# Idle products first, TensorE's and VectorE's early work in another order, and one weight split on GpSimd: a transformer stack on one core

## The reference

```python
z = (xn @ w_in).astype(jnp.float32)          # xn: x after rms_norm
q = z[..., :512]; k = z[..., 512:1024]; v = z[..., 1024:1536]   # per head of 64
u = z[..., 1536:]
q = partial_rope(q, positions) * (HEAD_DIM ** -0.5)
k = partial_rope(k, positions)
att = dilated_attention(q, k, v)
ssm = s5_mixer(u, a_re, a_im, log_dt, b_re, b_im, c_re, c_im, d_skip, w_glu)
y = jnp.concatenate([att, ssm], axis=-1)
return y @ w_out

# in s5_mixer, for 32 groups of 16 inputs and 64 complex states:
a_bar = jnp.exp(A * dt)
b_bar = ((a_bar - 1.0) / A)[..., None] * lax.complex(b_re, b_im)
bu = jnp.einsum('gpc,bsgc->bsgp', b_bar, u)
h = associative_scan over s of  h = a_bar * h + bu
y = jnp.einsum('gcp,bsgp->bsgc', c_mat, h).real + d_skip * u
y = gelu(y);  return y * sigmoid(y @ w_glu)
```

## Time and profile before

| what | value |
|---|---|
| median of 3 runs | 1249.65 us (1249.41 to 1251.18) |
| span of the profiled execution | 1248.4 us, first to last instruction |
| TensorE (PE) busy | 1236.7 us, 99% |
| VectorE (DVE) busy | 811.4 us, 65% |
| ScalarE (ACT) busy | 668.3 us, 54% |
| GpSimd (POOL) busy | 89.2 us, 7% |

### The profile page before, as it was taken

How to read it: one execution, slowest core, us unless ns; L and a number is a source line. 1 busy time by engine, 2 the same in 40 slices (tenths; PEclk the granted TensorE clock), 3 DMA queues, 4 the chain that set the end, 5 groups by cost and what they waited for, 6 DMA issues and landing times.

```text
span 1248.4 us, 15780 instructions
## 1 busy us (share of the span) xinstructions
PE 1236.7 (99%) x6366; PEld 1031.4 (83%) x6366; DVE 811.4 (65%) x1037; ACT 668.3 (54%) x965; POOL 89.2 (7%) x121
## 2 busy tenths in 40 slices
PE   7999999999999999999999999999999999999998
PEld 6778888888888888888888888888888888888887
DVE  7995756654788766554687746656547785655553
ACT  7865653433898654443687535444436644544431
POOL 2410000000100100000232000000001300000000
PEclk9999999999999999999999999999999999999999
DMA  7344555555554565555554235555555315555551
GB/s 306 105 140 144 190 198 172 199 173 199 189 200 163 192 222 183 192 179 200 181 199 169 68 102 169 202 192 179 184 192 181 131 39 202 199 186 185 183 188 67
DMA packets 32536, 216.60 MB, mean 173 GB/s; under 512 B 3904, under 2 KB 4544, under 8 KB 7376
## 3 DMA queue, kind: packets, MB, share of 16 engines
q1 hardware_dynamic: 30384, 210.32, 48.8%
q0 software_dynamic: 1360, 4.78, 1.2%
q10 hardware_dynamic: 720, 0.50, 0.1%
HBM read 214.54 MB, written 1.05 MB: 173 GB/s over the span
## 4 chain that ended last, share of the span: by engine, by line
PE 93%; DVE 4%; issue 1%; DMA 1%; ACT 0%; SPq 0%; DVEq 0%; ACTq 0%
PE PS L461 26%; PE PS L463 26%; PE PS L462 26%; PE PS L467 6%; PE PS L791 2%; PE PS L815 1%; PE PS L496 1%; PE PS L498 1%; PE PS L495 1%; PE PS L544 1%; PE PS L538 1%; PE PS L539 1%; DVE WL L1748 1%; DMA X<-in_x 1%; DVE YG L2037 1%
## 5 line engine op out<-in xcount | busy, mean ns | idle before, releaser
L1748 DVE TENSOR_TENSOR WL<-RAW,WH 128x2048 fp32r<-128x2048 f32 (+2 forms) x200 | 442.9, 2218 | 310.6 <-ACT WH L1130 310.6
L1130 ACT ACTIVATE WH<-RAW 128x2048 fp32r<-128x2048 f32 (+2 forms) x200 | 371.2, 1858 | 366.4 <-PE PS L463 366.1
L461 PE MATMUL PS<-WH,HTh 128*128 128x512 f32 (+1 forms) x848 | 334.6, 395 | 0.2
L463 PE MATMUL PS<-WH,HTl 128*128 128x512 f32 (+1 forms) x848 | 329.0, 388 | 0.0
L462 PE MATMUL PS<-WL,HTh 128*128 128x512 f32 (+1 forms) x848 | 328.3, 387 | 0.0
L463 PEld LDWEIGHTS PS<-WH,HTl 128*128 128x128 f32 x848 | 159.2, 188 | 33.2
L461 PEld LDWEIGHTS PS<-WH,HTh 128*128 128x128 f32 x848 | 159.4, 188 | 32.0 <-DVE WL L1748 0.8
L462 PEld LDWEIGHTS PS<-WL,HTh 128*128 128x128 f32 x848 | 159.5, 188 | 30.6
L461 PE MATMUL PS<-WH,YAh 128*128 128x512 f32 x402 | 158.6, 394 | 0.1
L463 PE MATMUL PS<-WH,YAl 128*128 128x512 f32 x402 | 156.7, 390 | 0.0
L462 PE MATMUL PS<-WL,YAh 128*128 128x512 f32 x402 | 156.5, 389 | 0.0
(11 more groups left out here) (354 smaller groups left out, 1442.9 us busy)
## 6 DMA issues: line engine op xcount, KB each, us to landing
RAW<-in_w SPq DMA_DIRECT2D x196, 1024.0 KB, 4.9
BC<-in_rows POOLq DMA_DIRECT2D x4, 512.0 KB, 4.0
YG<-in_mem POOLq DMA_DIRECT2D x4, 512.0 KB, 4.7
X<-in_x SPq DMA_DIRECT2D x2, 512.0 KB, 5.4
RAW<-in_w SPq DMA_DIRECT2D x4, 256.0 KB, 6.0
BC<-in_s SPq DMA_DIRECT2D x1, 512.0 KB, 11.6
YG<-in_s SPq DMA_DIRECT2D x1, 512.0 KB, 11.9
BB<-in_s SPq DMA_DIRECT2D x1, 512.0 KB, 12.5
```

Of the source, the lines that this page charges most:

```text
L461: e.matmul(out, ah, bh, start=start, stop=False)
L463: return e.matmul(out, al, bh, start=False, stop=stop)
L1130: e.activation(WH[:, c % NW, w], RAW[:, c % NR, w], ACT.Copy).then_inc(S.hi, 1)
L1748: e.tensor_tensor(WL[:, c % NW, w], RAW[:, c % NR, w], WH[:, c % NW, w].bitcast(f32), SUB).then_inc(S.lo, 1)
```

## The change

- **Idle products.** VectorE first sets 128x512 of YBh to 1.0 (S.warm). TensorE multiplies it into bank 7 nine times before the first turn and five times behind it; nothing reads the result.
- **first_edge in another order.** For chunk 0: the products upper by upper and lower by upper of the first row tile, then both halves of x's second turn, then what needs the weights' lower part, then the second row tile, with lower by upper last; the same for chunk 1.
- **ev_q.** u_turn stands behind k = 3 (it stood behind k = 2), b_turn behind k = 4 (k = 2), b_u(0) behind k = 6 (k = 3).
- **Chunk 3** is issued by SP ahead of YG and BB, copied by ScalarE ahead of the evacuation of u, and split by VectorE ahead of table(0) and late_c. Chunk 4 is issued ahead of cbias.
- **Chunk 4** (POOLED) is split by GpSimd, between row_rsqrt(0) and the CFe operations, signalled by S.plo; VectorE leaves it out, and `wait_lo` takes the place of the waits for S.lo.

The diff, cut to its core:

```diff
+        POOLED = (PLAN["ev_k"][0],)
+        def lo_n(c):
+            return c + 4 - sum(1 for p in POOLED if p <= c)
+        def wait_lo(e, c):
+            if c in POOLED:
+                e.wait_ge(S.plo, POOLED.index(c) + 1)
+            else:
+                e.wait_ge(S.lo, lo_n(c))
...
+            def idle_products(n):
+                for _ in range(n):
+                    e.matmul(PS[:, 7, :], YBh[:, 0, 0:128], YBh[:, 0:2, :].rearrange("p a b -> p (a b)"), start=True, stop=True)
...
             def first_edge():
...
+                def hi(t, k):
+                    ts, w = slice(128 * t, 128 * t + 128), slice(512 * (k % 4), 512 * (k % 4) + 512)
+                    e.wait_ge(S.hthi, htlo_n(0, t, k))
+                    e.matmul(PS[:, t, :], HTh[:, k, ts], WH[:, k // 4, w], start=k == 0, stop=False)
+                def lo(t, k):
+                    ts, w = slice(128 * t, 128 * t + 128), slice(512 * (k % 4), 512 * (k % 4) + 512)
+                    return e.matmul(PS[:, t, :], HTh[:, k, ts], WL[:, k // 4, w], start=False, stop=t == 0 and k == 7)
+                def rest(t, k):
+                    ts, w = slice(128 * t, 128 * t + 128), slice(512 * (k % 4), 512 * (k % 4) + 512)
+                    e.wait_ge(S.htlo, htlo_n(0, t, k))
+                    return e.matmul(PS[:, t, :], HTl[:, k, ts], WH[:, k // 4, w], start=False, stop=t == 1 and k == 7)
                 for k in range(4):
+                    e.wait_ge(S.hi, k + 1)
+                    hi(0, k)
+                    rest(0, k)
+                e.wait_ge(S.c_x1, 16)
+                turn(0, 1)
+                for k in range(4):
+                    e.wait_ge(S.lo, k + 1)
+                    lo(0, k)
+                for k in range(4):
+                    hi(1, k)
+                    lo(1, k)
+                for k in range(4):
+                    tk = rest(1, k)
                 tk.then_inc(S.used, 1)
+                e.wait_ge(S.hi1, 1)
+                for k in range(4, 8):
+                    if k == 6:
+                        e.wait_ge(S.hi, 5)
+                    hi(0, k)
+                    rest(0, k)
+                for k in range(4, 8):
+                    if k == 4:
+                        e.wait_ge(S.lo1, 1)
+                    elif k == 6:
+                        e.wait_ge(S.lo, 5)
+                    lo(0, k)
+                for k in range(4, 8):
+                    hi(1, k)
+                    lo(1, k)
+                for k in range(4, 8):
+                    tk = rest(1, k)
                 tk.then_inc(S.used, 1)
...
+            e.wait_ge(S.warm, 1)
+            idle_products(9)
             e.wait_ge(S.c_id, 16)
             e.wait_ge(S.c_x0, 16)
             turn(0, 0)
+            idle_products(5)
             first_edge()
...
-            rows_mm(PLAN["ev_q"], 4, 8, 512, HT, (2, 3), at={2: [u_turn, b_turn], 3: [b_first]})
+            rows_mm(PLAN["ev_q"], 4, 8, 512, HT, (2, 3), at={3: [u_turn], 4: [b_turn], 6: [b_first]})
...
             angles(0)
+            feed(PLAN["ev_u"][0])
             e.wait_ge(S.rs, RSTD["row0"])
             evac_in("ev_u", (0, 1), Qn)
-            feed(PLAN["ev_u"][0])
             pairs(0, uT, (4, 5))
...
+                    if n in POOLED:
+                        continue
...
+            e.memset(YBh[:, 0:2, :].bitcast(f32), 1.0).then_inc(S.warm, 1)
...
             late_b()
+            feed(PLAN["ev_u"][0])
             table(0)
-            late_c(lambda: feed(PLAN["ev_u"][0]))
-            rotate(0, lambda: feed(PLAN["ev_u"][1]))
+            late_c()
+            rotate(0)
+            feed(PLAN["ev_u"][1])
             table(1)
...
             row_rsqrt(0)
+            c = POOLED[0]
+            e.wait_ge(S.hi, c + 4)
+            e.tensor_tensor(WL[:, c % NW, :], RAW[:, c % NR, :], WH[:, c % NW, :].bitcast(f32), SUB).then_inc(S.plo, 1)
             e.wait_ge(S.pd, PD["CF"])
...
                 if c >= NR:
-                    e.wait_ge(S.lo, c + 1)
+                    wait_lo(e, c - NR)
...
             e.dma_start(tt[:, :], A["tab"][:, 640:896]).then_inc(S.c_t, 16)
+            weights(3)
             e.dma_start(YG[:, 0, :], A["s5"][:, 2048:3072]).then_inc(S.c_C, 16)
             e.dma_start(BB[:, :, :, :], A["s5"][:, 0:1024].rearrange("p (r q s) -> p r q s", r=2, q=4)).then_inc(S.c_B, 16)
+            weights(4)
             e.dma_start(cbias[:, :, :], A["tab"][:, 128:640].rearrange("p (t k) -> p t k", t=2)).then_inc(S.c_m, 16)
-            for c in range(NR, NCH):
+            for c in range(5, NCH):
                 weights(c)
```

More of the change, by code:

```diff
@@ L225 @@
     c_c c_id c_x0 c_x1 c_p c_i c_t c_B c_C c_m c_S c_bc c_tb c_gr c_mem c_o0 c_o1
-    fills half fin turn hthi htlo x yg sq var rs hi2 rowsq hsq
+    warm plo fills half fin turn hthi htlo x yg sq var rs hi2 rowsq hsq
     rsx th sg an fold yhi ylo
@@ L514, in first_edge @@
-                for i in range(4):
-                    e.wait_ge(S.lo, i + 1)
-                    e.matmul(PS[:, 0, :], HTh[:, i, 0:128], WL[:, 0, 512 * i:512 * i + 512], start=False, stop=False)
-                for k in range(4):
-                    tk = edge_product(0, 0, PS[:, 1, :], 1, k, slice(512 * k, 512 * k + 512))
-                tk.then_inc(S.used, 1)
[L520 to L526, removed]
+                def hi(t, k):
+                    ts, w = slice(128 * t, 128 * t + 128), slice(512 * (k % 4), 512 * (k % 4) + 512)
+                    e.wait_ge(S.hthi, htlo_n(0, t, k))
+                    e.matmul(PS[:, t, :], HTh[:, k, ts], WH[:, k // 4, w], start=k == 0, stop=False)
@@ L535, in rounded @@
                     if k % per == 0:
-                        e.wait_ge(S.lo, c + 4)
+                        wait_lo(e, c)
                     e.wait_ge(S.hthi, htlo_n(ed, 0, k))
@@ L1753, in feed @@
                     n = n_split[0]
+                    n_split[0] = n + 1
+                    if n in POOLED:
+                        continue
                     if ed:
@@ L1758, in feed @@
                     split_lo(n, slice(1024, CH) if ed else slice(0, CH))
-                    n_split[0] = n + 1
             def rest(out, src, hi, gain=None):
@@ L1979, in late_b, with late_c @@
                 e.tensor_tensor(AB[:, 1, :, :], AB[:, 1, :, :], CT_[:, 0, :, :], ADD).then_inc(S.pd, pd.up())
-            def late_c(then):
+            def late_c():
                 e.wait_ge(S.c_C, 16)
@@ L1987, in late_c @@
                 e.tensor_tensor(CT_, CC[:, :, :, :], fi, MUL).then_inc(S.pd, pd.up())
-                then()
                 e.wait_ge(S.pd, PD["f2"])
```

## The result

The change is slower: the median is **1255.12 us** (1254.97 to 1256.61, 5 runs) against 1249.65 us (1249.20 to 1251.18, 5 runs), a ratio of 1.0042 (95% interval 1.0029 to 1.0054), so 5.5 us more. 1254.0 us had been predicted. The profiled spans are 1253.2 and 1248.4 us, 4.8 us apart. On record a time stands 1.75 to 1.95 us above the span of the same execution, so the profiled execution before took some 1250.2 us, half a us more than the median: the medians are further apart than the spans. The ratios leave out three slow executions of over 1370 us, one of the kernel with small CFe operations and two of the kernel before.

A forecast was written before the change was run, and what follows sets the result against it. The prediction took VectorE's chain without slack, then TensorE, to bound the kernel. Terms +0.9, -2.6, -1.1, +1.1 and +6.1 gave +4.4 us, added to the 1249.65 median: 1254.0 us, range 1248.4 to 1257.0.

The forecast's parts named there:

- Start and ev_q: TensorE's start: idle products raise its clock sooner, ev_q begins at 21.3 instead of 24.34, but b_u(0) ends 0.9 us later.
- The rival without an earlier clock: At the start: idle products don't raise the clock sooner, ev_q stays at 24.3; +7.4 us, 1257.0; chance 0.06.
- The split on GpSimd: Chunk 4's split on GpSimd starts at about 35.0 and takes 3.4 us, so chunk 4 is ready at 38.4.
- my bound of 4.2: Chunk 4's split on GpSimd: four operations of 1.05 us would be 4.2 us, the upper split time in the range.
- TensorE's lead: At ev_k: of the 3.0 us TensorE gains by ev_q, some 1.1 are left after waiting for chunk 4.
- the hold of L2071: VectorE's operation ready at 37.3 (L2027 before) waits until GpSimd finishes chunk 4 at 38.4: +1.1 us.
- The CFe operations: Six GpSimd operations behind chunk 4's split, each between two of VectorE's next, hold up VectorE's chain: +6.1 us.
- The sum: VectorE's chain, L2020 to L2042: b_u(0) +0.9, split gone -2.6, L2522 no longer ahead -1.1, L2027 +1.1, CFe +6.1; together +4.4.
- The wait ahead of c_h(0): c_h(0) needs CFe and W, so TensorE waits some 3 to 4 us ahead of it.
- The rival with free scans: VectorE's scans are not held up, only four CFe operations cost: 2.0 us less, +2.4, 1252.0; chance 0.12.
- The rival without hold-up: GpSimd's operations cost VectorE nothing, TensorE sets the pace: 1248.5, or 1247 with a split of 2.3 us; chance 0.25.
- the relay: VectorE's chain from L2020 (34.12) to the split at 71.03 has no slack, then TensorE takes over; any delay delays the end.

The follow-up runs named there:

- the kernel with small CFe operations: The change with each of the six CFe operations cut to 128x64, the rest of CFe set to zero at the start: 1254.28 us, ratio 1.0035.
- the version above: The change without GpSimd's split, old places in ev_q, GpSimd's CFe and rope work put where VectorE reads PSUM: 1247.40 us, ratio 0.9979.
- the pair with whole and small operations: The change with u_turn, b_turn, b_u(0) at their old places: whole CFe operations 1253.66 us, ratio 1.0030; cut to 128x64 1248.03 us, ratio 0.9984.
- VectorE's split with old and with new places: The change with VectorE splitting chunk 4: u_turn, b_turn, b_u(0) at old places 1249.92 us, ratio 0.9999; at new places 1251.81 us, ratio 1.0022.
- keeping TensorE busy: The change with VectorE splitting chunk 4 and 12 more idle products ahead of ev_k: 1250.63 us, ratio 1.0007.

## Why the prediction was right, step by step

- **Start and ev_q.** ev_q at 21.01 (21.3 predicted), L2064 at 34.97 and GpSimd's start at 34.99 (34.9 to 35.0 and 35.0): right. The clock came up sooner than I took it. The rival without an earlier clock is refuted: it had ev_q at 24.3, and even without idle products it began at 22.59.
- **The split on GpSimd: mis-sized.** I took 3.4 us from the line through two smaller operations, and it took 4.56 (4.56 to 4.63 in the six runs that have it ahead of whole or small CFe operations): twice VectorE's 2.29, above my bound of 4.2 too. The Trainium skill ("GPSIMD Engine Reference", 4.1 Engine selection) states about twice VectorE's time for two inputs; these runs agree with it, and the estimate of 4.6 us that I worked out from it and did not use was right. The line through two small operations did not hold for one four times as large. So nothing of TensorE's lead was left at ev_k, where I had kept 1.1 us, and the hold of L2071 was 2.1 us (37.43 to 39.55, the split's end) instead of 1.1.
- **The CFe operations.** VectorE's own pace from L2071 to W is 8.7 us (the version above), and it took 14.2: held up by 5.5 us, where I had 6.1.
- **The sum** then is 0.9 - 2.6 - 1.1 + 2.1 + 5.5 = +4.8 us; W was 4.7 us late, and so was the split at the end of the chain. The +4.4 came out near it because two errors of 1.0 and 0.6 us had opposite signs: that is luck, though the terms and their order were right. The median moved by 5.5 us. The 0.7 us between that and the spans' 4.8 are not in the sum: I added to the median what I had read from an execution half a us longer than it.
- **The wait ahead of c_h(0)** came, but was 2.2 us in two parts (1.97 for L2085, 0.22 for L2086) and not 3 to 4: TensorE had come to ev_k 1.1 us later than I had it.
- **The rival with free scans** is refuted: two scans took 3.99 us beside CFe, and 2.33 without it, before and in the version above. The rule of the Trainium skill ("SBUF — State Buffer", Who interferes with whom) that two SBUF inputs decide holds for scans too in this trace.
- **The rival without hold-up** is refuted by the pair with whole and small operations, 5.6 us apart in time, and by VectorE's rows beside CFe.
- **Missing in the prediction** was the second path, through direct_terms and ScalarE. In the change it is hidden: direct_terms stood at 45.12, and VectorE's second TN had no idle time before it. It decides once the first path is shortened: of the 1.9 us between VectorE's split with old and with new places (1249.9, 1251.8) keeping TensorE busy brought back 1.2. The prediction had looked at what TensorE's wait costs, not at what its clock does after it.

## What to carry to other kernels

Count work that you give to GpSimd against VectorE's rows too: in these runs an operation with two SBUF inputs on GpSimd cost VectorE nothing while VectorE read PSUM or waited, and held it up where VectorE had two SBUF inputs itself. Look at what is queued behind a moved operation, since here it was the six operations behind the split, not the split, that cost most. And a lead that one engine wins is worth what the next engine in the relay can take over: the new start brings TensorE to ev_q 3.3 us earlier in the change, and alone it made no difference in time (ratio 0.9995). Last, read a profile together with the time of its own execution: two of those above stood 2.4 and 3.2 us over the median of their kernel.

## What the runs showed of the hardware that I had not expected

TensorE's clock fell in the middle of the kernel: after idle times of 3.49 and 6.23 us the products came 0.43 us apart, and after 3.08 us they did in the runs with small CFe operations and without idle products, while after 3.09 us in the profiled execution of the change they stayed at 0.23. The same length of wait thus cost the clock in one execution and not in another. Nor did it take a long wait:

```profile
32.39 0.63 PE L463 MATMUL PS<-WH,HTl 128*128 128x512 f32 x1
```

This row is of the run with the new start alone. There the products came 0.43 us apart from 32.39 to 35.38, behind the small matmuls of b_u(0) and a wait of only 0.59 us ahead of them. Behind the small matmuls of another b_u and a wait of 0.60 us it fell again in the run without idle products, at 71.95, and there it cost 1.6 us. In the profile of the kernel before the granted clock reads 1.00 in every stretch. So a profile shows one of several courses, and executions of one kernel differ by it: with the old places and VectorE's split three at a mean granted clock of 0.999 took 1250.9 to 1251.4 us, eight at 1.000 took 1249.3 to 1250.1. What decides when it falls no run shows.

Here the granted clock of the stretches shows the fall (the column ahead of the DMA share); in the run with CFe ahead of the split it was

```profile
36.00:44.00 8.00, 1.77 (x5) 1.17 (x4) 7.90 (x6) 3.27 (x4) 6.51 (x3) 0.76 0.07 10
44.00:52.00 8.00, 7.93 (x42) 6.06 (x40) 7.83 (x7) 2.88 (x9) 0.00 (x0) 0.50 0.70 254
```

0.50 is the lower of the two levels. In the first 13 us of the run without idle products it reads 1.00 although the products are 0.43 us apart there: at this kernel's start the distance of the products has to be read. With twelve idle products in the wait the clock stayed up in all eleven executions.
